# One column slab of a hybrid decoder layer moved ahead of the HGRN queries, and the mixing phases begun one slab later (Trainium2, one core)

## The reference

```
z = rms_norm(x) @ w_in       # q, kc, vc, ks, vs, kw, vw, gates, SiLU paths, pooling values, HGRN q/f/i, merge gates
o_a = nsa_mixer(...)         # attention: compressed (kc, vc), selected (ks, vs) and window (kw, vw) keys
o_b = pool_mixer(...)        # causal means over 2, 4, 8, 16 tokens, then a 256x256 matrix for each group
o_c = hgrn2_mixer(...)       # gated linear recurrence, 8 heads of 128, f = lb + (1-lb)*sigmoid(f_logits)
merged = sum(sigmoid(merge_b) * ((o_b * silu_b) @ w_branch[b]))
x + rms_norm(merged @ w_out)
```

## Time and profile before

| | before |
|---|---|
| median of 3 runs | 511.75 us (511.73 to 512.19) |
| span of the profiled execution | 510.2 us |
| PE busy | 492.7 us, 97% |
| DVE busy | 361.2 us, 71% |
| ACT busy | 252.5 us, 50% |
| POOL busy | 164.4 us, 32% |
| HBM traffic | 149 GB/s over the span |

### The profile page before, as it was taken

One profiled execution on the slowest core, in us unless ns is written; L12 is line 12 of the kernel. 1 busy time (PEld: TensorE's weight loads), 2 busy tenths in 40 slices (PEclk: granted clock), 3 DMA queues, 4 the chain that ended last, 5 costly groups with the idle time before them and its releaser, 6 DMA issues.

```text
span 510.2 us, 9851 instructions
## 1 busy us (share of the span) xinstructions
PE 492.7 (97%) x4034; PEld 474.5 (93%) x4034; DVE 361.2 (71%) x675; ACT 252.5 (50%) x369; POOL 164.4 (32%) x169
## 2 busy tenths in 40 slices
PE   4999969999999999999999999999999999999995
PEld 4999969999999999999999989989999999999995
DVE  4869896999999776798697356577546437645663
ACT  6845515236375363764356354466645335434441
POOL 1008910250640000997037362556457220000000
PEclk9999959999999999999999999999999999999999
DMA  9955432423445465455527432252434555568502
GB/s 299 318 169 170 159 114 84 133 49 108 146 130 166 126 173 133 148 174 167 166 82 248 139 111 84 85 164 87 163 103 147 166 164 166 192 202 309 166 0 84
DMA packets 77032, 76.46 MB, mean 150 GB/s; under 512 B 6783, under 2 KB 75775, under 8 KB 76987
## 3 DMA queue, kind: packets, MB, share of 16 engines
q1 hardware_dynamic: 76699, 75.64, 47.6%
q10 hardware_dynamic: 288, 0.18, 0.1%
HBM read 74.77 MB, written 1.05 MB: 149 GB/s over the span
## 4 chain that ended last, share of the span: by engine, by line
PE 91%; POOL 3%; DVE 2%; ACT 2%; DMA 1%; issue 0%; DVEq 0%
PE ps L952 69%; PE ps L980 5%; PE ps L1132 3%; POOL R L341 2%; PE ps L1081 1%; PE ps L1067 1%; PE ps L1148 1%; POOL R L343 1%; PE ps L981 1%; PE ps L1100 1%; PE ps L978 1%; DMA R<-x 1%; DVE R L632 1%; PE ps L1086 1%; PE ps L1156 1%; PE ps L995 1%
## 5 line engine op out<-in xcount | busy, mean ns | idle before, releaser
L952 PE MATMUL ps<-hH,WL 128*128 128x256 f32 x696 | 201.2, 289 | 0.0
L952 PE MATMUL ps<-hL,WH 128*128 128x256 f32 x696 | 197.7, 284 | 0.0
L952 PE MATMUL ps<-hH,WH 128*128 128x256 f32 x696 | 197.7, 284 | 0.0
L591 DVE TENSOR_TENSOR WL<-W,WH 128x2048 fp32r<-128x2048 f32 x66 | 152.6, 2311 | 20.4 <-PE ps L952 19.8
L411 ACT ACTIVATE WH<-W 128x2048 fp32r<-128x2048 f32 x66 | 124.4, 1888 | 68.1 <-PE ps L952 67.8
L952 PEld LDWEIGHTS ps<-hH,WL 128*128 128x128 f32 x696 | 132.9, 191 | 1.0 <-issue 0.7
L952 PEld LDWEIGHTS ps<-hL,WH 128*128 128x128 f32 x696 | 132.8, 191 | 0.8 <-issue 0.7
L952 PEld LDWEIGHTS ps<-hH,WH 128*128 128x128 f32 x696 | 132.8, 191 | 0.0
L341 POOL TENSOR_TENSOR R<-R 128x256 f32<-128x256 f32 x32 | 32.8, 1030 | 83.3 <-PE ps L983 55.4
L372 POOL TENSOR_SCALAR R<-R,st 128x256 f32<-128x256 f32 x32 | 29.2, 925 | 81.5 <-DVE st L764 81.5
L952 PE MATMUL ps<-bH,WL 128*128 128x256 f32 x192 | 55.2, 287 | 0.0
(11 more groups left out here) (190 smaller groups left out, 803.3 us busy)
## 6 DMA issues: line engine op xcount, KB each, us to landing
W<-w_in SPq DMA_DIRECT2D x49, 1024.0 KB, 5.2
W<-w_branch SPq DMA_DIRECT2D x12, 1024.0 KB, 5.2
W<-w_out SPq DMA_DIRECT2D x4, 1024.0 KB, 5.3
R<-x SPq DMA_DIRECT2D x2, 512.0 KB, 4.5
W<-w_in SPq DMA_DIRECT2D x2, 512.0 KB, 6.6
R<-cmp_w SPq DMA_DIRECT2D x2, 512.0 KB, 8.0
OC<-pool_w SPq DMA_DIRECT2D x4, 256.0 KB, 6.1
R<-x SPq DMA_DIRECT2D x1, 1024.0 KB, 7.2
```

The lines of the kernel that those rows point to most:

```text
L591: dve.tensor_tensor(WL[:, s % 2, :, 0:n], W[:, s % 3, :, 0:n], WH[:, s % 3, :, 0:n], ALU.subtract).then_inc(s_lo, 1)
L952: mm = pe.matmul(o, l, r, start=(k == 0 and j == 0 and not (split and c)), stop=(k == KC - 1 and j == 2 and not (split and not c)))
```

## The change

`kc` becomes slab 4. The HGRN queries and values move from slabs 4 to 11 to slabs 5 to 12; `vc` and all that follow keep their numbers. The constants `U0`, `CK`, `CV`, `CX`, `SC`, `TURN` and `H0` go up by one; `G0` stays. ACT's logarithms stay at slab 4 and the DVE's scans at slabs 4 to 7. The POOL loop begins at slab 32 as before, so that it still meets the first branch slab.

```
-    out = [("f", n, "in", C_HF + n * SLAB) for n in range(4)]
+    out = [("f", n, "in", C_HF + n * SLAB) for n in range(4)] + [("kc", 0, "in", C_KC)]
     for n in range(4):
         out += [("hq", n, "in", C_HQ + n * SLAB), ("hv", n, "in", C_HI + n * SLAB)]
-    out += [("kc", 0, "in", C_KC), ("vc", 0, "in", C_VC), ("vs", 0, "in", C_VS), ("vw", 0, "in", C_VW),
+    out += [("vc", 0, "in", C_VC), ("vs", 0, "in", C_VS), ("vw", 0, "in", C_VW),
...
-U0 = 9
-CK, CV, CX, SC, TURN = 27, 28, 29, 31, 34
-H0 = 32
+U0 = 10
+CK, CV, CX, SC, TURN = 28, 29, 30, 32, 35
+H0 = 33
 G0 = 36
...
-            for s in range(H0, NS):
+            for s in range(WHERE[("branch", 0, 2)], NS):
...
-                if s == U0 - 5:
+                if s == 4:
```

## The result

The changed kernel takes 517.35 us (median of 4 runs, 516.29 to 517.86) against 511.74 before: slower by 1.07%, ratio 1.0107 with a 95% interval of 1.0092 to 1.0122. The forecast was 514.9 us, slower, with a range up to 518.5. The profiled execution has a span of 515.9 us against 510.2, so 5.7 us more.

The account below looks back on a forecast made before the run. One 4.8 us PE wait, for head 0 before the first unit's scores, was the only one behind the start. -8.45 + 1.8 + 5.4 + 2.9 + 1.5 = +3.15 us: 511.75 to 514.9 us, range 512.0 to 518.5, own range 513.4 to 516.3.

Parts of the forecast that it names:

- rival 2: The clock is also lost at the last pair's squares (Term C): 1.75 + 1.9 us more, 518.5 us; chance 0.12.
- Rival 5: The wait is only traded: `kc` read contends, product 6 and all behind it 3.3 us later, 518.2 us; chance 0.05.
- the old wait: PE's 4.8 us wait at the first HGRN unit's scores for head 0; with its half clock 8.45 us, nearly all removed.
- Term A: The start: DVE's 3.35 us `kc` read at slab 4 delays products 6 to 10 and head 0; costs 1.8 us.
- Term B: Unit 6, slab 16: head 4's multiplications slowed beside POOL's fourth pair, delaying unit 8's scores and product 18; costs 5.4 us.
- Term C: Last pair's sums of squares: L1025 waits as the `ks` read lies ahead of DVE's last copy; costs 2.9 us.
- The clock: PE's clock taken as lost behind Term B's waits, costing 1.5 us, and as kept at Term C's gap.
- Rival 1: The clock is kept in Term B: 513.4 us; chance 0.27.
- Rivals 3 and 4: 3: Term B doesn't happen, 508.0 us, chance 0.10. 4: Term C doesn't, 512.0, or 510.5 with clock kept, chance 0.08.

## Why the prediction was right, and where its numbers were off

The direction was right, by the stalls that were named for it, and the time lies in the stated range. But it lies outside the forecast's own range of 513.4 to 516.3, 2.45 us above the forecast and near the times of rivals 2 (518.5) and 5 (518.2), which only the rows tell apart.

**That the old wait would go.** Right. Its clock loss went with it, and slab `kc` filled the place.

**Term A, 1.8 us.** Mechanism right, size too small by 0.9. The read of `kc` took 3.34 us beside POOL, as the earlier trace rows had it, and the page of the Trainium skill "SBUF — State Buffer", in its rules on the shared port pair, agrees. From there DVE's round set the pace, as the sum said: the `lo`s of slabs 6 to 9 ended at 46.27, 52.45, 58.40 and 64.47, rounds of 6.07 us on average against the sum's 6.05. But the first of them ended 0.3 us late, so that product 9 began at 64.52 instead of 64.2. Then six of head 0's operations were slow instead of five, so that unit 0's scores began at 70.85 instead of 70.1 and product 10 at 73.65 instead of 72.9. The last 0.2 is product 10 itself, which lasted 6.0 us in the chain where the sum had 5.75. A product that PE begins out of a standstill takes that much here: its second matmul starts 0.22 us after the first (64.52 and 64.74), where it is 0.12 further on.

The sentence "The clock survives: no single gap reaches 1 us" held in the profiled runs of the changed kernel and of two others with the same start, and failed in those of three (the gate slab at 17, `lo(27)` first, and both together again): two short gaps were followed by a loss of about 1.4 us. In the run with `vs` at slab 4 I had put most of the waits down to the place of the `kc` read. That was wrong. The kernel with POOL held back showed that they come from POOL's second pair.

**Term B, 5.4 us.** Mechanism right in every part: removed by holding POOL back, removed by moving the gate slab, and made in the kernel before by moving it there. Measured 3.95. DVE began head 4 0.85 us before POOL instead of 0.45 (128.37 and 129.22), so that five operations instead of two were fast. Three operations at 0.42 less are 1.3 us, most of the difference of 1.45. The sum had a slip besides: 9.2 and twice 2.25 are 13.7, not 13.9, so that its own terms give 5.2. Its upper bound was also too low, since all 16 operations at 0.69 give 7.2 and not 6.5.

**Term C, 2.9 us.** Right, 3.1 measured, and both removed and made alone. (Its upper bound, 2.35 and 0.75, is 3.1 and not 3.2.)

**The clock.** Right for B (1.6 against 1.5). Wrong for C: "in C the gap of 2.9 is hardly longer than 2.6 and alone; I take it as kept". It was lost, which makes 2.8 us, and is the failing term of the sum: the clock behind C was put at nothing. With it the sum is 517.7, near the 517.35 measured, but that it comes so near is in part luck, since A was 0.9 too small and B 1.45 too large. The loss was rival 2, with a chance of 0.12, when the same observation (a fall 2.6 us into a gap) was used for one gap and not for the other. That observation was no fixed limit: the clock fell 2.0 us into C's gap, and in B 3.0 us after PE had run dry, when it was at work again. The Trainium skill, "TensorE: Matmul & The Clock Gate", in its part on oscillation, has the clock fall at every wait for data of a kernel whose waits take 3 to 5 us; B's 2.3 and C's 3.1 us are at or below the lower end of that, and in the changed kernel's profile the clock fell at both.

Nor has the loss one size or come every time. Behind the same wait of 3.1 us at L1025 it was 2.8 us in the changed kernel and 1.7 to 1.8 in three others (POOL waiting, the gate slab at 17, and `ks` at 24). Of the kernel with `lo(27)` first, whose profile still has B's gap of 2.3 us, two runs had a mean clock of 1.00 and took 510.73 and 510.89 us, while in the profiled one the clock fell both at that gap and between 73 and 74 us, and it took 513.2. Those two were not profiled. What decides between these outcomes no run here shows.

**The rivals.** Rival 1, the clock kept in B: no, it fell. Rival 2, the clock lost in C as well: this is what happened. Rivals 3 and 4, that B or C would not happen: neither. Rival 5, that the read of `kc` would contend: no, 3.34 us.

## What to carry to other kernels

A slab number that serves as the clock of all engines doesn't move a phase as a whole: what is pinned to other numbers (a short slab, an expensive read) changes partners, and each new pair has to be checked against the margin that the old one had, here 0.25 us at L1025. When two engines slow each other inside SBUF, hold back the one without a deadline: it costs one wait instruction, and here it gained 4.1 us by itself, where the move of `kc` with its two repairs gained 5.4 and all together 7.2. Check the next item that it then falls on. A stall of PE of 2 or 3 us is to be priced with the half clock behind it, which here was mostly 0.6 to 0.9 of the wait again.

## What the runs showed of the hardware that I had not expected

- The clock of PE fell in some executions of one program and not in others behind gaps of 0.33 and 0.7 us within 3 us (507.8 and 506.3 us), and two runs of a kernel whose profile has a gap of 2.3 us had a mean clock of 1.00 (510.73 and 510.89 us). Kernels with such gaps took times in clusters about 1.5 us apart (506.2 and 507.8 us, 511.1 and 512.5 us), while the version with no gap over 0.2 us spread over 0.6 us in 4 runs.
- Beside POOL each of DVE's small operations with both inputs in SBUF started every 0.62 us instead of every 0.20, whatever its stage in the kernel, so that starting head 0 earlier by 2.9 us ended it only 0.7 us earlier.
- Behind one and the same wait of 3.1 us the half clock cost 2.8 us in one kernel and 1.7 to 1.8 in three others.
